# Samples' delta rule on 32-wide selectors and 32-row updates, and narrow front products in column halves and 32x32 blocks

## The reference

```python
proj = x @ w_in                                  # q, k, v, z and the two gates per head
qkv_c = silu(causal_dwconv(qkv, conv_w))
q, k = l2norm(q), l2norm(k)                      # 8 heads of 128
beta = sigmoid(b);  g = -exp(a_log) * softplus(a + dt_bias)
# per token:  S_t = a_t S_{t-1} + beta_t k_t (v_t - a_t S_{t-1}^T k_t)^T,   o_t = S_t^T q_t,   a_t = exp(g_t)
o = rms_norm(o) * norm_g * silu(z);   y = o @ w_out
```

## Time and profile before

| | us |
|---|---|
| median of 3 runs | 1750.44 (1749.59 to 1751.86) |
| the profiled execution's own time | 1752.5 |
| its span, first to last instruction | 1749.1 |
| block 1 | 0 to 264.9 |
| block 2 | 264.9 to 398.6, the samples' levels from 348.3 |
| block 3 | 398.6 to 1749.1 |

### The profile page before, as it was taken

How to read it: one execution, slowest core, us unless ns; L and a number is a source line. 1 busy time by engine, 2 the same in 40 slices (tenths; PEclk the granted TensorE clock), 3 DMA queues, 4 the chain that set the end, 5 groups by cost and what they waited for, 6 DMA issues and landing times. The chain is left out here.

```text
span 1749.1 us, 22019 instructions
## 1 busy us (share of the span) xinstructions
PE 1715.6 (98%) x7827; PEld 1334.3 (76%) x7827; DVE 1088.8 (62%) x2090; ACT 460.1 (26%) x1084; POOL 254.5 (15%) x540
## 2 busy tenths in 40 slices
PE   8999999999899999999999999999999999999999
PEld 6777778877677777777777777777677777777777
DVE  4766775667867666672437655467666667632365
ACT  2433407730422222220014101114222222200051
POOL 0111216762210000000100000002000000001100
PEclk9999999999999999999999999999999999999999
DMA  4232210312122222241130223211222222322211
GB/s 153 73 114 86 80 61 14 110 52 106 48 82 77 83 73 73 85 154 66 67 110 25 96 85 94 73 50 49 61 84 73 73 85 80 129 101 74 82 53 55
DMA packets 45644, 139.36 MB, mean 80 GB/s; under 512 B 4945, under 2 KB 12241, under 8 KB 45537
## 3 DMA queue, kind: packets, MB, share of 16 engines
q1 hardware_dynamic: 42864, 133.36, 23.1%
q10 hardware_dynamic: 2672, 4.61, 0.8%
HBM read 129.63 MB, written 8.31 MB: 79 GB/s over the span
## 5 line engine op out<-in xcount | busy, mean ns | idle before, releaser
L274 PE MATMUL bank<-z,ring 128*128 128x288 f32 x1952 | 508.7, 407 | 6.9 <-DVE z L392 2.3
L274 PEld LDWEIGHTS bank<-z,ring 128*128 128x128 f32 x1952 | 371.1, 191 | 113.4 <-issue 5.1
L274 PE MATMUL bank<-x,ring 128*128 128x288 f32 x1632 | 429.7, 410 | 10.5 <-DMA x<-in_x 4.8
L274 PEld LDWEIGHTS bank<-x,ring 128*128 128x128 f32 x1632 | 311.2, 192 | 101.8 <-issue 6.7
L2188 DVE SCALAR_TENSOR_TENSOR scratch<-scratch 128x592 f32<-128x592 f32 x176 | 146.2, 832 | 25.6 <-ACT scratch L2132 24.0
L274 PE MATMUL bank<-y,ring 128*128 128x288 f32 x616 | 156.7, 406 | 0.3 <-DVE x L1949 0.3
L274 PEld LDWEIGHTS bank<-y,ring 128*128 128x128 f32 x616 | 117.0, 190 | 33.0 <-issue 0.7
L274 PE MATMUL bank<-big,ring 128*128 128x288 f32 x536 | 137.0, 411 | 2.7 <-issue 1.1
L274 PEld LDWEIGHTS bank<-big,ring 128*128 128x128 f32 x536 | 102.4, 192 | 33.1 <-issue 3.4
L2222 POOL COPY scratch<-scratch 128x2 f32<-128x2 f32 x88 | 26.5, 301 | 467.7 <-ACT scratch L2118 467.7
L2132 ACT ACTIVATE scratch<-scratch 128x592 f32<-128x592 f32 x88 | 69.4, 789 | 90.6 <-DVE scratch L2162 89.0
(11 more groups left out here) (377 smaller groups left out, 2236.3 us busy)
## 6 DMA issues: line engine op xcount, KB each, us to landing
ring<-in_w_up SPq DMA_DIRECT2D x88, 512.0 KB, 3.5
ring<-in_w_scin SPq DMA_DIRECT2D x24, 512.0 KB, 3.6
ring<-in_w_qkv SPq DMA_DIRECT2D x21, 512.0 KB, 3.5
ring<-in_w_down SPq DMA_DIRECT2D x12, 704.0 KB, 4.3
scratch<-in_w_down SPq DMA_DIRECT2D x12, 704.0 KB, 5.3
ring<-in_w_z SPq DMA_DIRECT2D x8, 512.0 KB, 3.5
big<-in_st_S SPq DMA_DIRECT2D x16, 256.0 KB, 5.6
out_dn_S_sample<-big SPq DMA_DIRECT2D x16, 256.0 KB, 2.3
```

The source lines that it names most:

```text
L274: last = pe.matmul(bank[:, 0:HALF], w[:, k * P:(k + 1) * P], rhs(k), start=start and k == 0, stop=k == self.depth - 1, skip_group_check=no ...
```

## The change

In the front, `half_of_array` moves the second column half of the gate logits and of the norm sums to array columns and PSUM partitions 64 on, with everything that reads them there. `grams_pe` computes only the four 32x32 blocks of each chunk and head, each from a weight of 128 rows and 32 columns on its own quarter of the array's columns (128 matmuls instead of 32), one bank per chunk, the wait for the roots now ahead of the third chunk, and DVE multiplies by chunk (16 instructions of 32x256 instead of 32 of 32x128).

In the samples, the selectors become 32 wide: `states_pe` makes 16 matmuls per head, each with a 32-column weight, into four quarters of the array (k and q by samples 0 to 3 and 4 to 7). The values are no longer multiplied by the decays: ACT multiplies k instead (`keys_act`, 4 copies of 64x128 per head), with the last decays gathered by two small DVE copies, and `update_pe` makes 8 matmuls per head of 32 rows by 128 columns, on row quarters 0 and 1 in turn, into the two banks of `UPDATE_BANKS`. POOL's three memsets of padding go, and those of the selectors shrink from 1024 to 640 columns. DVE's adds, POOL's decays and SP's stores go head by head; turns and gates go by groups of four heads; the order of PE's list behind the levels is new.

```diff
-        GROUP, SH, SLOT_N, DIAG = 4, NB // 2, 3, 2 * SAMP + NS
+        GROUP, SH, SLOT_N = 4, NB // 2, 3
+        SEL_STEP = BL + NS
...
         def sel_own(h, x):
 
 
-            at = SEL_AT[h % SLOT_N] - SAMP
-            own = SCR[:, at:at + NB * DIAG].rearrange("p (b x) -> p b x", b=NB)
-            return own[:, :, SAMP * (1 + x):SAMP * (1 + x) + NS]
-
-        def sel_window(h, b):
-            at = SEL_AT[h % SLOT_N] + 2 * SAMP * b
-            return SCR[:, at:at + 2 * SAMP]
+            at = SEL_AT[h % SLOT_N] + NB * SEL_STEP * x
+            return SCR[:, at:at + NB * SEL_STEP].rearrange("p (b c) -> p b c", b=NB)[:, :, 0:NS]
+
+        def sel_window(h, b, x):
+            at = SEL_AT[h % SLOT_N] + NB * SEL_STEP * x + SH * SEL_STEP * (b // SH) + BL * (b % SH)
+            return SCR[:, at:at + BL]
...
+        def sample_quad(r):
+            return slice(BL * r, BL * (r + 1))
+
+        def keys(h):
+            return Y[A, h, 0:SH * P].rearrange("p (b n) -> p b n", b=SH)
+
+        LAST_S = scratch(2560, H, SH)
+        UPDATE_BANKS = ((0, 1), (2, 3), (0, 1), (2, 3), (4, 5), (6, 7), (2, 3), (4, 5))
+
+        def nth_update(h, r):
+            return 2 * h + r + 1
...
             def states_pe(self, pe, h):
                 pe.wait_ge(self.state_in[h], 32)
                 pe.wait_ge(self.sel, 2 * h + 2)
-                for b in range(NB):
-                    last = pe.matmul(SBANK[h][:, P:2 * P], sel_window(h, b), states(h, b // SH)[:, b % SH, :],
-                                     start=b == 0, stop=b == NB - 1)
+                for i in range(SH):
+                    for r in range(2):
+                        for x in range(2):
+                            last = pe.matmul(SBANK[h][sample_quad(2 * x + r), P:2 * P], sel_window(h, SH * r + i, x),
+                                             states(h, r)[:, i, :], start=i == 0, stop=i == SH - 1)
                 last.then_inc(self.ks, 1)
...
-                pe.matmul(SBANK[h][:, :], S_KTOK[:, h, :], decayed(h, r), start=True, stop=True).then_inc(self.su, 1)
-
-            def turn_pe(self, pe, h):
-                pe.wait_ge(self.scaled, h // GROUP + 1)
-                pe.wait_ge(self.s_out, updates(h, 1))
-                pe.transpose(SBANK[h][:, 0:SAMP], S_OS[B, h, :], IDENT[B, B]).then_inc(self.o_turned, 1)
+            def update_pe(self, pe, h):
+
+
+                pe.wait_ge(self.keyed, h + 1)
+                for b in range(SH):
+                    for r in range(2):
+                        part = sample_quad(r)
+                        last = pe.matmul(SBANK[UPDATE_BANKS[h][r]][:, b * P:(b + 1) * P], keys(h)[part, b, :],
+                                         S_VNEW[part, h, :], start=True, stop=True)
+                        if b == SH - 1:
+                            last.then_inc(self.su, 1)
+
+            def turn_pe(self, pe, group):
+                pe.wait_ge(self.scaled, group + 1)
+                for h in range(group * GROUP, (group + 1) * GROUP):
+                    last = pe.transpose(SBANK[group][:, h % GROUP * SAMP:(h % GROUP + 1) * SAMP], S_OS[B, h, :], IDENT[B, B])
+                last.then_inc(self.o_turned, 1)
...
+                for h in range(FILL[-1] + 1):
+                    self.values_pe(pe, h)
...
+                for h in range(GROUP):
+                    self.outputs_pe(pe, h)
                 pe.wait_ge(self.prompt.gated, (NCH - 1) * 2 + 2)
                 self.states_pe(pe, 7)
+                self.values_pe(pe, 6)
+                self.values_pe(pe, 7)
+                pe.wait_ge(self.o_sq, 2)
+                self.update_pe(pe, 0)
+                pe.wait_ge(self.o_sq, 4)
+                self.update_pe(pe, 1)
+                for h in range(GROUP, H):
                     self.outputs_pe(pe, h)
+                pe.wait_ge(self.s_out, nth_update(0, 1))
+                self.update_pe(pe, 2)
+                pe.wait_ge(self.s_out, nth_update(1, 1))
+                self.update_pe(pe, 3)
+                pe.wait_ge(self.o_sq, 6)
+                self.update_pe(pe, 4)
+                pe.wait_ge(self.s_out, nth_update(2, 0))
+                self.turn_pe(pe, 0)
+                pe.wait_ge(self.o_sq, 8)
+                self.update_pe(pe, 5)
+                pe.wait_ge(self.s_out, nth_update(2, 1))
+                self.turn_pe(pe, 1)
+                pe.wait_ge(self.s_out, nth_update(3, 1))
+                self.update_pe(pe, 6)
+                pe.wait_ge(self.s_out, nth_update(4, 1))
+                self.update_pe(pe, 7)
...
-            def values_dve(self, dve, h):
-                dve.wait_ge(self.vn, h + 1)
-                dve.tensor_tensor(decayed(h, 0)[A], S_VNEW[A, h, :].unsqueeze(1).to_broadcast([SAMP, SH, P]),
-                                  S_DEC[A, h, last_tok][:, 0:SH].unsqueeze(2).to_broadcast([SAMP, SH, P]),
-                                  ALU.mult).then_inc(self.vb0, 1)
-
-            def update_dve(self, dve, h, r):
-                dve.wait_ge(self.su, updates(h, r))
-                dve.wait_ge(self.sdec, updates(h, r))
-                dve.tensor_tensor(states(h, r), states(h, r), SBANK[h][:, :].rearrange("p (b n) -> p b n", b=SH),
-                                  ALU.add).then_inc(self.s_out, 1)
-
-            def gate_dve(self, dve, h):
-                dve.wait_ge(self.o_turned, h + 1)
-                dve.scalar_tensor_tensor(out=smp(3 * h + 1), in0=SBANK[h][:, 0:SAMP], scalar=norm_g,
-                                         in1=Z[:, h, SEQ:TOK], op0=ALU.mult, op1=ALU.mult).then_inc(self.o_gated, 1)
+            def update_dve(self, dve, h):
+                for r in range(2):
+                    dve.wait_ge(self.su, nth_update(h, r))
+                    dve.wait_ge(self.sdec, nth_update(h, r))
+                    dve.tensor_tensor(states(h, r), states(h, r),
+                                      SBANK[UPDATE_BANKS[h][r]][:, :].rearrange("p (b n) -> p b n", b=SH), ALU.add
+                                      ).then_inc(self.s_out, 1)
...
+                for h in range(GROUP + 1):
+                    self.update_dve(dve, h)
...
+            def keys_act(self, act, h):
+                for b in range(SH):
+                    last = act.activation(keys(h)[:, b, :], S_KTOK[A, h, :], ACT.Copy, scale=LAST_S[A, h, b:b + 1])
+                last.then_inc(self.keyed, 1)
...
+                act.wait_ge(self.last, 2)
+                act.wait_ge(self.tok, 2 * H)
+                for h in range(H):
+                    self.keys_act(act, h)
+                for h in range(FILL[-1] + 1):
+                    self.values_act(act, h)
+                for h in range(GROUP):
+                    self.outputs_act(act, h)
+                for h in range(FILL[-1] + 1, H):
+                    self.values_act(act, h)
+                for h in range(GROUP, H):
+                    self.outputs_act(act, h)
...
-            def decay_pool(self, pool, h, r):
+            def decay_pool(self, pool, h):
                 pool.wait_ge(self.ks, h + 1)
-                pool.tensor_tensor(states(h, r), states(h, r),
-                                   S_EG[:, h, last_tok][:, SH * r:SH * (r + 1)].unsqueeze(2).to_broadcast([P, SH, P]),
-                                   ALU.mult).then_inc(self.sdec, 1)
...
+                self.decay_pool(pool, 0)
                 self.select_pool(pool, 5)
-                self.decay_pool(pool, 1, 0)
+                self.decay_pool(pool, 1)
                 self.select_pool(pool, 6)
-                self.decay_pool(pool, 2, 0)
+                self.decay_pool(pool, 2)
...
+                for h in range(3, 6):
+                    self.decay_pool(pool, h)
...
                 self.scale_pool(pool, 0)
...
+                self.decay_pool(pool, 6)
...
                 self.scale_pool(pool, 1)
...
+                self.decay_pool(pool, 7)
...
+        def half_of_array(half, part):
+
+            return BANK[6 + half][64 * half + part.start:64 * half + part.stop]
...
-                    last = pe.matmul(BANK[6 + half][0:40, 0:HALF], WBA[:, k, :], X[:, k, half * HALF:(half + 1) * HALF],
+                    last = pe.matmul(half_of_array(half, slice(0, 40))[:, 0:HALF], WBA[:, k, :], X[:, k, half * HALF:(half + 1) * HALF],
...
-                    last = pe.matmul(BANK[6 + half][rows, cols.start - half * HALF:cols.stop - half * HALF], sum_column(m),
+                    last = pe.matmul(half_of_array(half, rows)[:, cols.start - half * HALF:cols.stop - half * HALF], sum_column(m),
...
         def grams_pe(pe, some):
-            for q in range(NCH * H)[some]:
-                c, h = q // H, q % H
-                k = BIG[:, 3 * h, c * CH:(c + 1) * CH]
+            for c in some:
                 pe.wait_ge(q_silu, 4 * NPAIR)
-                if q >= 8:
+                if c >= 2:
                     pe.wait_ge(rooted, 3)
-                if q >= 16 and q % 4 == 0:
-                    pe.wait_ge(kkd, q - 12)
```

(73 more changed lines are left out.)

105 lines of the change are left out of this document (26 added, 79 removed).

## The result

The changed kernel takes **1735.28 us** in the median (4 runs, 1734.23 to 1735.66), beside 1750.21 us for the kernel before in the same comparison: ratio 0.9912, 95% interval 0.9895 to 0.9929. The forecast was 1729 with a range of 1723 to 1741. So it is faster, by 14.9 us where 21.7 were forecast; the median lies inside the range, and outside the forecast's own 1725 to 1733. The profiled execution took 1735.66, its span is 1733.6 against 1749.1.

What follows compares the result with a forecast made beforehand. PE was taken to bound the front, DVE the samples' tail. Front -8.9, samples -13.8 and clock +1.0 gave -21.7 us: 1729 us beside the 1750.44 median; own range 1725 to 1733, stated range 1723 to 1741.

Steps and rivals of the forecast that it cites:

- Overlap on all 128 rows: Narrow products on PE: those using all 128 rows run fully beside each other, a round costing one record's time.
- Gate logits: Start of the front: halves save 3.9 us, but the wait for u1 leaves only 0.7 us, with PE idle some 2.5 us.
- Grams: End of the front: 64 records at 7.1 us become 64 rounds of 0.033 us, 2.1 us, so 5.0 us less.
- Rival 1: Products on 128 rows: narrow weight loads not hidden, state product 1.95 us, total -7.2 us, 1743 us; chance 0.15.
- rival 2: Products on 128 rows: no overlap at all, state product 4.0 us, total +10.2 us, 1761 us; chance 0.07.
- Samples: The samples' delta rule: shorter state products and no multiplies on DVE end it at 384.4 instead of 398.2, 13.8 us earlier.
- A second fall of the clock inside the samples: Sign of being wrong: the granted clock falling again within the samples' delta rule; no size given.
- Front: 0 to 264.9 us: z tiles 8.9 us earlier, less 1.0 us for a clock fall near 24 us.
- z(2) starts at 208.2: End of the front: this z tile starts at 208.2 instead of 217.15, 8.9 us earlier, and all z tiles with it.
- rival 3: One part gains nothing (sample updates don't overlap, POOL late, or Gram loads stay slow): each +5 us, 1734 us; chance 0.16.
- Rival 4: End of the front: DVE's chain becomes the last, costing 1 to 2 us, inside the forecast's range; no separate chance.
- That loss stays: Start of block 3: half clock behind the idle time before it keeps costing 1.7 us in the new kernel.

Runs made afterwards that it cites:

- spread kernel: The changed kernel with the Gram products of chunks 1 to 3 spread between z tile products and two banks swapped; 1729.38 us, ratio 0.9878.
- the last one: The changed kernel plus spread Gram products, extra matmuls before u1 and behind the last sample update, and stores split over SP and ACT; 1728.64 us, ratio 0.9869.
- whole gates: The changed kernel, but with the gate logits as before, both halves on array columns 0 to 39; 1734.61 us, ratio 0.9902.
- the filled gap: The changed kernel with spread Gram products and five extra matmuls in PE's idle time before u1; 1730.10 us, ratio 0.9879.

## Why the prediction was right, and where it was not

**Overlap on all 128 rows (right).** Gate logits 4.08 us (forecast 4), a q tile's sums 0.60 (0.58), Grams 0.76 a chunk (0.73 with what a record takes to come out), state products 1.01 (1.14). Rival 1 wanted 1.95 for a state product and rival 2 4.0; both are out. The rule of the Trainium skill behind rival 1 (page "TensorE: Matmul & The Clock Gate", Part 3) was no guide here: weight loads of 128 rows by 32 columns ran beside products on the same rows, 32 loads in 0.81 us within the 1.08 of a state product.

**Samples (right, 13.2 of 13.8).** State products, level times, first add and the adds' length came nearly as worked out. Two terms came out worse. The block starts 0.91 us behind the last add (383.83 - 382.92), where it was 0.42 behind the last gate before: SP issues the last store behind the last add, for 0.33 us, which I had passed over with "spread over 11 us", 0.5. And the adds took 0.4 longer, since the last updates came late under the half clock from 378.6 on; where it fell only 1.8 us before their end (spread kernel) or not at all (the last one), the adds take 11.1 us, 0.2 less than forecast. The earlier first add gave 0.3 of it back, and 0.5 + 0.4 - 0.3 is the 0.6. The two small copies were mis-sized too, 1.30 us and not 0.3 (L990), but PE waited only 0.2 for DVE there. "A second fall of the clock inside the samples" was named as a sign of being wrong, and it came; it cost 0.6 us (11.7 against 11.1).

**Front (direction right, 7.9 forecast, 1.6 measured).** The ledger, from z starts and ends: up to z(0) -2.4 (192.36 to 189.96), z(0) to z(1) -1.7, z(1) to z(2) +0.7, from there to the last copy +1.8. The steps:
- *Norm sums:* 0.47 us a q tile, as forecast. Right.
- *Gate logits:* "0.7 survives" holds only while the clock holds. With its fall z(0) is 1.06 later than with whole gates. I had put 1.0 on that fall; it costs 1.7. So whole gates would have been 1.1 better here, and without the fall the halves are 0.6 better; which of the two comes is a matter of the execution.
- *Grams:* **the failed step is "z(2) starts at 208.2".** It counted the records' time and the wait for the roots (0.3; measured 0.67), and held the instructions to be there when wanted. 192 narrow records in a row were faster than their code: 3.06 us.
- *Clock behind it:* 1.7 us that no step of mine had, in this execution. The spread kernel, free of gap, root wait and this fall, won 5.3.

3.06 + 0.4 + 1.7 + (1.7 - 1.0) = 5.9 of the 6.3 us; the last 0.4 I can't place. The rest of the sum held: in the kernel with chunk 0's Grams twice, whose execution had neither the gap nor a fall in the front, the front ends at 256.73, 8.2 us earlier than before, with 64 records (0.5 us) more to do. That is the 8.9 to 0.2 us.

**The number.** 1735.3 is 6.3 us above 1729 and outside the forecast's own 1725 to 1733. It lies in the stated range because that was stretched over rival 3, and what filled the space was none of the rivals. That part of being right is luck.

**Rivals.** The median lies beside rival 3's 1734, but none of its mechanisms is what happened: updates on two row places overlap (32 records in 2.05 us are 1 us an update), POOL was in time, and the loads of the Grams are not what bound them. A number that fits is no evidence for the story beside it. Rival 4 (DVE's chain last) didn't come to it: the chain ended at 256.8, 6.3 us before the last copy, and 1.4 before it in the spread kernel.

**Clock at block 3.** "That loss stays" was right in effect and wrong in reason: with a full clock there the product that waits for DVE starts no earlier, 13.9 us behind the block's start as before, since DVE's queue covers it. It was no loss before either, since that product waited for DVE then too (0.30 us).

## What to carry to other kernels

When products become so narrow that a record costs 0.01 us instead of 0.1, count the instructions: a stretch that burned a block of code in 1.3 us ran dry, and the view shows it as "issue" idle time in the middle of one instruction group. Mix such products with wide ones; the order costs nothing and was worth 5.3 us of the front here, 1.7 of them a fall of the clock that not every execution has. And be wary of a gain in front of a wait: the idle time that it makes can cost more, by the clock, than what was saved. Leaving the work there or filling the gap ended the front 1.2 and 1.8 us earlier in the traces, which the medians don't show, and at the samples' end a fill only moved the idle time to the next wait.

## What the runs showed of the hardware that was not expected

- PE's code comes in 16 KB blocks, one for about 125 records, and the place where PE stops moves with the code: 125, 109 and no stop with 0, 16 and 64 records more ahead. The stop lasted 2.5 to 3.3 us in five executions, and the block's packet came 0.2 to 0.6 us behind its start.
- The granted clock fell to half for 3.4 us behind 5 of 6 gaps of 2.40 us, with the same code up to there and the same gap in the sixth. At the samples' end it stayed low for 6.8 or 10.2 us, where before it was 3.4.
- Issuing one of the samples' stores cost SP 0.33 us or up to twice that: 0.33 to 0.65 within the changed kernel's last eight, 0.63 to 0.72 for all eight with the filled gap. What makes the difference was not found.
